# RWKV-7 recurrence on one core: key, value and inverse blocks turned by 128x128 transposes instead of 64x64 identity products

## The reference, cut to what matters

```python
def _wkv7_step(S, inp):
    r, decay, k, v, a_vec, b_vec = inp
    sa = jnp.einsum('bhij,bhj->bhi', S, a_vec)
    S = S * decay[:, :, None, :] + sa[..., None] * b_vec[:, :, None, :] + v[..., None] * k[:, :, None, :]
    return S, jnp.einsum('bhij,bhj->bhi', S, r)
```

## Time and profile before

| | |
|---|---|
| median of 3 runs | 2178.58 us (2175.6 to 2179.8) |
| the profiled execution | 2177.06 us, its span 2175.3 us |
| PE busy, share of the span | 2003.1 us, 92% |
| PE matmuls in the program | 21990 |
| recurrence, first to last product | 1210.5 to 1457.3 us |

### The profile page before, as it was taken

One profiled execution on the slowest core, in us unless ns is written; L12 is line 12 of the kernel. 1 busy time (PEld: TensorE's weight loads), 2 busy tenths in 40 slices (PEclk: granted clock), 3 DMA queues, 4 the chain that ended last, 5 costly groups with the idle time before them and its releaser, 6 DMA issues. The chain is left out here.

```text
span 2175.3 us, 49311 instructions
## 1 busy us (share of the span) xinstructions
PE 2003.1 (92%) x21990; PEld 1893.9 (87%) x21990; DVE 1164.1 (54%) x1603; ACT 535.1 (25%) x967; POOL 201.8 (9%) x272
## 2 busy tenths in 40 slices
PE   8998988998999999996999766768999999999996
PEld 8996768996999999994989666657998899999996
DVE  5346775554655555338558533326664565555333
ACT  2005774113201010002238332324222211010000
POOL 4000001000200000110000433310010100000010
PEclk9999999999999999997999999998999999999998
DMA  4244212351222223221221000014341122222331
GB/s 130 78 129 129 59 30 78 117 165 58 83 87 86 86 87 89 83 87 51 84 63 49 8 4 4 5 30 116 113 160 54 58 80 87 86 86 85 89 89 58
DMA packets 299350, 169.87 MB, mean 78 GB/s; under 512 B 10312, under 2 KB 294160, under 8 KB 299184
## 3 DMA queue, kind: packets, MB, share of 16 engines
q1 hardware_dynamic: 294960, 151.25, 24.0%
q10 hardware_dynamic: 4224, 16.12, 1.9%
HBM read 155.94 MB, written 11.41 MB: 77 GB/s over the span
## 5 line engine op out<-in xcount | busy, mean ns | idle before, releaser
L259 PE MATMUL psum<-words_r,weights_high_r 128*128 128x272 f32 (+1 forms) x7808 | 1495.1, 291 | 12.3 <-DVE words_r L210 5.0
L259 PEld LDWEIGHTS psum<-words_r,weights_high_r 128*128 128x128 f32 x7808 | 1234.6, 190 | 24.2 <-issue 20.2
L259 PE MATMUL psum<-words_r,weight_ring_r 128*128 128x272 f32 (+1 forms) x3904 | 1132.2, 290 | 0.0
L259 PEld LDWEIGHTS psum<-words_r,weight_ring_r 128*128 128x128 f32 x3904 | 738.7, 189 | 0.0
L205 DVE TENSOR_SCALAR weights_high_r<-weight_ring 128x1024 fp32r<-128x1024 f32 (+1 forms) x258 | 177.9, 689 | 519.8 <-PE psum L259 515.8
L210 DVE TENSOR_TENSOR weight_ring_r<-weight_ring,weights_high_r 128x1024 fp32r<-128x1024 f32 (+1 forms) x264 | 319.4, 1210 | 10.1 <-ACT weights_high_r L344 1.2
L399 POOL TENSOR_TENSOR words<-words,words 128x544 f32<-128x544 f32 x42 | 75.5, 1798 | 1445.7 <-ACT words L386 1445.7
L1804 ACT ACTIVATE words<-words 128x544 f32<-128x544 f32 x44 | 29.0, 659 | 451.7 <-DVE words L1745 451.7
L2557 PE MATMUL psum<-words 64*64 64x64 f32 (+1 forms) x3296 | 94.0, 235 | 26.8 <-issue 23.4
L376 DVE TENSOR_TENSOR words<-psum,words 128x544 f32<-128x544 f32 x48 | 34.8, 725 | 141.7 <-PE psum L259 141.7
L2557 PEld LDWEIGHTS psum<-words 64*64 64x64 f32 x3296 | 78.1, 139 | 30.7 <-issue 27.4
(11 more groups left out here) (316 smaller groups left out, 1904.3 us busy)
## 6 DMA issues: line engine op xcount, KB each, us to landing
weight_ring<-in_ffn_w_gate_up_dram SPq DMA_DIRECT2D x88, 512.0 KB, 3.8
weight_ring<-in_xa_w_kv_dram SPq DMA_DIRECT2D x32, 512.0 KB, 3.9
weight_ring<-in_ffn_w_down_dram SPq DMA_DIRECT2D x32, 448.0 KB, 3.4
weight_ring<-in_sb_w_qkv_dram SPq DMA_DIRECT2D x24, 512.0 KB, 3.8
weight_ring<-in_xa_w_q_dram SPq DMA_DIRECT2D x16, 512.0 KB, 3.6
weight_ring<-in_xa_w_o_dram SPq DMA_DIRECT2D x16, 512.0 KB, 3.6
weight_ring<-in_ffn_w_down_dram SPq DMA_DIRECT2D x16, 512.0 KB, 3.6
weight_ring<-in_sb_w_o_dram SPq DMA_DIRECT2D x8, 512.0 KB, 3.7
```

Of the source, the lines that this page charges most:

```text
L259: last = nc.tensor.matmul(c.psum[0:job.m(u), job.bank(q) + h, 0:w], weights[:, k, :], x[:, k, h * w:(h + 1) * w], start=job.opens(u) and k ...
```

## The change

`turn_b`, `turn_k`, `turn_v` and the turning half of `join` no longer use `by_head`. Two tiles of a quad that lie side by side (128 columns) are turned by one transpose of a 128x128 matrix, so that two instructions take the place of eight. The results lie in another order, row tile 2j+h instead of 2h+j, which the new `of_rows` reads; DVE writes `z.q` through `by_pair` in place of `by_side`. [...] The space for `v_in` comes from `to64`, which is now written over `am`; ACT's next copy into `am` waits for `join64_done` in place of `to64_ready`.

```diff
-        self.b_end, self.k_end = take(L), take(L)
+        self.b_end, self.k_end, self.v_in = take(L), take(L), take(L)
...
-        self.m8, self.am, self.to16, self.to32, self.to64 = (take(L) for _ in range(5))
+        self.m8, self.am, self.to16, self.to32 = (take(L) for _ in range(4))
+        self.to64 = self.am
...
             def to64(i):
                 for z, e in both:
-                    if i:
-                        pool.wait_ge(e["join64_done"], i)
-                    nc.gpsimd.tensor_tensor(z.to64, z.am, spread(c.to64_lo, L), ALU.mult).then_inc(e["to64_ready"], 1)
+                    pool.wait_ge(e["to16_ready"], i + 1)
+                    pool.wait_ge(e["to32_ready"], i + 1)
+                    nc.gpsimd.tensor_tensor(z.to64, z.am, spread(c.to64_lo, L), ALU.mult).then_inc(e["to64_ready"], 1)
+
+            def v_in(i):
+                for z, e in both:
+                    if i:
+                        pool.wait_ge(e["v_turned"], i)
+                    nc.gpsimd.tensor_copy(z.v_in, v_pairs(i)[:, z.pairs, 0:L]).then_inc(e["v_in_ready"], 1)
...
                 b_end(i)
+                v_in(i)
                 m1_and_i(i)
...
-                    nc.vector.tensor_copy(by_side(z.q), slot(q, 1)).then_inc(e["q8_ready"], 1)
+                    nc.vector.tensor_copy(by_pair(z.q), slot(q, 1)).then_inc(e["q8_ready"], 1)
...
-                    nc.vector.tensor_tensor(by_side(z.q), slot(q, x), by_side(z.q), ALU.add).then_inc(e[ready], 1)
+                    nc.vector.tensor_tensor(by_pair(z.q), slot(q, x), by_pair(z.q), ALU.add).then_inc(e[ready], 1)
...
                     act.wait_ge(e["m8_ready"], i + 1)
                     if i:
-                        act.wait_ge(e["to64_ready"], i)
+                        act.wait_ge(e["join64_done"], i)
...
+            def turn(q, x, t):
+
+                for j in range(2):
+                    done = tr(c.psum[:, 4 * q + 2 * x + j, 0:P], t[:, 2 * j:2 * j + 2, :].rearrange("p a n -> p (a n)"), c.ident[:])
+                return done
+
+            def of_rows(t):
+
+                return lambda h, p, j: t[:, 2 * j + h, :]
...
-                    by_head(slot(q, 0), paired(z.k_end), "h", ident, "p").then_inc(e["k_turned"], 1)
+                    turn(q, 0, z.k_end).then_inc(e["k_turned"], 1)
...
             def turn_v(i):
                 for q, (z, e) in enumerate(both):
+                    pe.wait_ge(e["v_in_ready"], i + 1)
                     pe.wait_ge(e["q16_ready"], i + 1)
                     if q == 0 and i == 1:
                         pe.wait_ge(first, 2)
-                    by_head(slot(q, 1), v_of(z, i), "h", ident, "p").then_inc(e["v_turned"], 1)
+                    turn(q, 1, z.v_in).then_inc(e["v_turned"], 1)
...
             def join(q, x, z, to):
-                turned, crossed = (c.psum[:, 4 * q + 2 * x:4 * q + 2 * x + 2, n * P:(n + 1) * P].rearrange("p b (j n) -> p b j n", j=2) for n in range(2))
-                by_head(turned, of_p(z.q), "p", ident, "h")
-                return by_head(crossed, of_p(to), "p", of_p(z.q), "h", start=False)
+                for j in range(2):
+                    tr(c.psum[:, 4 * q + 2 * x + j, P:2 * P], z.q[:, 2 * j:2 * j + 2, :].rearrange("p a n -> p (a n)"), c.ident[:])
+                return by_head(slot(q, x), of_p(to), "p", of_rows(z.q), "h")
```

More of the change, by code:

```diff
@@ L2257, in wkv @@
              "am_copied b_rows_ready k_rows_ready v_rows_ready m2t_ready x_ready join16_ready join32_ready join64_ready w_ready y_ready "
-             "b_end_ready k_end_ready m1i_ready m2i_ready to16_ready to32_ready to64_ready faded_ready").split()
+             "b_end_ready k_end_ready v_in_ready m1i_ready m2i_ready to16_ready to32_ready to64_ready faded_ready").split()
     s = [{x: c.sem(f"wkv{q}_{x}") for x in names} for q in range(2)]
@@ L2282, in tokens, with v_pairs @@
         return t[:, z.pairs, column(i):column(i) + w]
+    def v_pairs(i):
+        return c.flat(1, 6 * REGION)[:, 4 * REGION + column(i):5 * REGION + column(i)].rearrange("p (k t) -> p k t", k=PAIRS)
     def decay(z, i):
@@ L2287, in wkv @@
     wide = c.flat(1, 6 * REGION).rearrange("p (r n) -> p r n", r=6)
-    r_words, v_words = (c.flat(1, 6 * REGION)[:, r * REGION:(r + 1) * REGION + DEC] for r in (2, 4))
+    r_words = c.flat(1, 6 * REGION)[:, 2 * REGION:3 * REGION + DEC]
     def spread(m, n):
@@ L2570, in of_h @@
                 return lambda h, p, j: t[:, 2 * p + j, :]
-            def ident(h, p, j):
-                return c.ident64
             def at(z, h, p, j, i):
@@ L2579, in r_of @@
                 return lambda h, p, j: r_words[:, at(z, h, p, j, i):at(z, h, p, j, i) + L]
-            def v_of(z, i):
-                return lambda h, p, j: v_words[:, at(z, h, p, j, i):at(z, h, p, j, i) + L]
+            def turn(q, x, t):
[4 more added lines that the diff above has]
+                return lambda h, p, j: t[:, 2 * j + h, :]
             def scores(dst, lhs, z, i):
@@ L2616, in turn_b @@
                         pe.wait_ge(e["x_ready"], 1)
-                    by_head(slot(q, 0), paired(z.b_end), "h", ident, "p").then_inc(e["b_turned"], 1)
+                    turn(q, 0, z.b_end).then_inc(e["b_turned"], 1)
             def turn_k(i):
@@ L2668, in join @@
             def join(q, x, z, to):
-                turned, crossed = (c.psum[:, 4 * q + 2 * x:4 * q + 2 * x + 2, n * P:(n + 1) * P].rearrange("p b (j n) -> p b j n", j=2) for n in range(2))
-                by_head(turned, of_p(z.q), "p", ident, "h")
-                return by_head(crossed, of_p(to), "p", of_p(z.q), "h", start=False)
+                for j in range(2):
+                    tr(c.psum[:, 4 * q + 2 * x + j, P:2 * P], z.q[:, 2 * j:2 * j + 2, :].rearrange("p a n -> p (a n)"), c.ident[:])
+                return by_head(slot(q, x), of_p(to), "p", of_rows(z.q), "h")
             def joined(q, x, z):
                 kept = z.join.rearrange("p (b j) n -> p b (j n)", b=2)
-                return by_head(slot(q, x), lambda h, p, j: kept[:, p, j * L:(j + 1) * L], "h",
-                               lambda h, p, j: kept[:, p, P + j * L:P + (j + 1) * L], "p")
+                return by_head(slot(q, x), lambda h, p, j: kept[:, j, P + p * L:P + (p + 1) * L], "h",
+                               lambda h, p, j: kept[:, p, j * L:(j + 1) * L], "p")
             def join16(i):
@@ L2719, in w @@
                     pe.wait_ge(e["v_rows_ready"], i + 1)
-                    by_head(slot(q, 0), of_p(z.far[:, :, 0:L]), "p", of_p(z.v_rows), "p").then_inc(e["w_begun" if i else "w_done"], 1)
+                    by_head(slot(q, 0), of_p(z.far[:, :, 0:L]), "p", of_rows(z.v_rows), "p").then_inc(e["w_begun" if i else "w_done"], 1)
                 for q, (z, e) in enumerate(both):
@@ L2732, in u @@
                     pe.wait_ge(e["w_ready"], i + 1)
-                    by_head(slot(q, 1), of_p(z.q), "p", of_p(z.w), "p").then_inc(e["u_done"], 1)
+                    by_head(slot(q, 1), of_rows(z.q), "p", of_p(z.w), "p").then_inc(e["u_done"], 1)
             def y_known(i):
@@ L2737, in y_known @@
                     pe.wait_ge(e["u_ready"], i + 1)
-                    by_head(slot(q, 1), of_p(z.v_rows), "p", of_p(z.far[:, :, L:]), "h").then_inc(e["y_begun"], 1)
+                    by_head(slot(q, 1), of_rows(z.v_rows), "p", of_p(z.far[:, :, L:]), "h").then_inc(e["y_begun"], 1)
                 for q, (z, e) in enumerate(both):
@@ L2754, in s_known @@
                         pe.wait_ge(e["x_ready"], i + 2)
-                    by_head(slot(q, 0), of_p(z.k_rows), "p", of_p(z.v_rows), "h")
+                    by_head(slot(q, 0), of_rows(z.k_rows), "p", of_rows(z.v_rows), "h")
             def s_solved(i):
                 for q, (z, e) in enumerate(both):
-                    by_head(slot(q, 0), of_p(z.b_rows), "p", of_p(z.u), "h", start=False).then_inc(e["s_done"], 1)
+                    by_head(slot(q, 0), of_rows(z.b_rows), "p", of_p(z.u), "h", start=False).then_inc(e["s_done"], 1)
             def state_rows():
```

## The result

The changed kernel takes 2144.44 us (median of 4 runs, 2142.49 to 2146.69) against 2179.01 us for the kernel before (4 runs, 2175.6 to 2179.8): a ratio of 0.9845 with a 95% interval of 0.9828 to 0.9862. The forecast was 2141 us. The profiled execution took 2144.70 us, its span 2143.0, 32.3 us less than the span before.

A forecast was written before the change was run, and what follows sets the result against it. The prediction took the recurrence's code length, fetched in 256-instruction packets, as the bound. 52.3 packets at 4.0 us give 209.2 us instead of 246.8, so 2177.06 - 37.6 = 2139.5, plus 1.5 for the median: 2141 us, range 2128 to 2161.

The forecast's parts named there:

- The bound: In the recurrence, PE runs through a 256-instruction packet in 2.73 us, but the next comes only after 3.86 us.
- The count of instructions: PE in the recurrence: 108 turns fall from 32 to 4 instructions, net 3006 fewer; 64 packets become 52.3.
- The array's work: PE's array in the recurrence: busy time stays about 175 us, at best 1.5 us less.
- I take 0.108, from the row of the same form: PE's turns in the recurrence: transposes stand 0.108 us apart, 0.216 us for the two of a turn.
- The upper end: PE's turns, if each transpose stood alone with its load: 0.413 us each, adding 64 us of busy time.
- The distance: Time from packet to packet in the recurrence: 4.0 us taken, so 52.3 packets last 209.2 us, 37.6 us less.
- the 0.14 us above the mean: Allowance in the recurrence's packet time, 4.0 against 3.86 us, for packets with more work and hand-overs no pause hides.
- Pauses still 256 instructions apart: Expected sign on PE in the recurrence afterwards: pauses at every 256 instructions, unnamed waiting down from 66 to 25 to 35 us.
- What would cover it: POOL's two added copies per chunk fall into its idle time and cost nothing; without that cover, 11 us.
- That the pauses are not the code's: Rival: PE's pauses in the recurrence are dependences the profile fails to name; time stays at 2178.6 us; chance 0.05.
- That waits take the place of half of the pauses: Rival: hand-overs between PE, ACT and DVE hold a chunk near 25.3 us; 2160 us; chance 0.13.
- The low clock: Rival: the recurrence runs at granted clock 0.50 throughout, 253 us, making the kernel slower, 2185 us; chance 0.04.

The follow-up runs named there:

- the second profile: The changed kernel, unaltered, run again on another occasion beside a version with reordered joins: 2147.15 us, ratio 0.9874 to the kernel before.
- before_wide: The kernel before with identity products of turns and joins streaming 128 columns in place of 64, same instruction count: 2177.95 us against 2176.93, ratio 1.0002.
- before_split: The kernel before with each identity product of turns and joins split into two of 32 columns, so more instructions: 2225.81 us, ratio 1.0230.

## Why the prediction was right, point by point

*The bound.* "The code's length bounds the stage, not the array and not the dependences" was right for the kernel before, and by two runs shown: 17.5 us of array work cost nothing, and with 14 packets more the stage took 47.5 us more, with 3.9 us for 256 instructions before and 3.7 with the split at full clock.

*The count of instructions.* It came out to the unit: 20478 matmuls, 290 operations on POOL, 52 packets in the stage.

*The array's work.* Here a term was mis-sized. The step "I take 0.108, from the row of the same form" took the distance of eight transposes in a row for pairs between quarter products. A pair took 0.37 us in place of 0.216, and the group behind it 0.39 in place of 0.23; PE was busy for 182.27 us, and 178.06 in the second profile, in place of 175. The upper end, 0.413 us for each transpose, was too far: a pair took less than one such.

*The distance.* 217.0 us over 52 packets are 4.17 us, in the second profile 211.9 / 52 = 4.08; forecast were 4.0. The stage was 7.8 us above the forecast 209.2 in the first profile, with its 13.6 us of low clock, and 2.7 us above in the second, where the mean clock was 0.99. What I had put into the 0.14 us above the mean, packets whose own work is longer, is what the trace has. This window of the changed kernel holds 1070 instructions, four packets and a bit, with one pause of more than 0.4 us, at its end (1.20 us, to 1303.15):

```profile
1286.10:1303.10 17.00, 15.19 (x535) 12.63 (x535) 5.93 (x15) 7.47 (x18) 6.77 (x12) 1.00 0.02 4
```

It is 4.07 us for 256, with 3.6 us of them busy. "Pauses still 256 instructions apart" was thus too simple for the kernel after: its stage is now partly bound by its own work; how much of the 0.17 us above 4.0 is clock and how much the changes between array and quarters, the two profiles don't separate.

*What would cover it.* POOL's copies were hidden as said (idle time ahead of line 2342: 43.1 us left of 67.8), no wait for POOL shows on PE, and DVE's sums by pairs took no longer (419 ns against 420).

*The rivals.* That the pauses are not the code's is excluded by `before_wide` and `before_split` together. That waits take the place of half of the pauses did not happen: PE's waits for DVE and ACT are 4.1 us. The low clock did not make the kernel slower (its mean in the stage was 0.97 and 0.99, before 0.98), but it was nearer to the matter than I had it: before, 256 instructions at the low clock took 3.96 us, hardly more than a packet's 3.86, while now they take 6.7 us in the window of 10.2 us above, and the stage gets longer by it.

## What to carry to other kernels

When an engine's pauses come at a fixed number of instructions and the instruction queue moves one packet for each, count instructions, not microseconds of work: two whole-array transposes in place of eight quarter products are worth it even where the array gains nothing. Look in the trace for the place where code runs without a loop and faster than one packet in some 4 us. Once the code no longer bounds the stage alone, an order in which whole-array and quarter work change seldom may bring a little more: here 7 us, with overlapping intervals.

## What the runs showed of the hardware that was not expected

A pair of transposes between groups of quarter products took 0.37 us and the group behind it 0.39, while 0.216 was measured in a row of eight transposes and 0.23 among groups. Products of one bf16 column between float32 groups left PE busy for 425.21 of 425.30 us and at a granted clock of 0.50 throughout, 0.77 us for a group and its padding. The distance between packets hardly depended on how many there were: 3.92 us for 63 (246.8 / 63), 3.82 for 77 (294.3 / 77).
